# RWKV-7 features: the key norm's root, turn and spreads moved between the gate sigmoids, with one PSUM place for the spreads

## What is computed

```python
w_log = -jax.nn.softplus(-(w0 + jnp.einsum('bldr,drc->bldc', jnp.tanh(lw), w2))) - 0.5
decay = jnp.exp(-jnp.exp(w_log))
a = jax.nn.sigmoid(a0 + jnp.einsum('bldr,drc->bldc', la, a2))
gate = jax.nn.sigmoid(lg) @ g2
kk = l2_normalize(heads(k * k_k))          # t * rsqrt(sum(t*t) + eps), per head of 64 channels
k_dir = k[:, :, None, :] * (1.0 + (a - 1.0) * k_a)
...
y = y + jnp.sum(r * k_dir[:, :, d] * u[d], axis=-1, keepdims=True) * v     # the bonus, d = 0, 1
```

## Time and profile before

| | |
|---|---|
| median of 3 runs | 4022.79 us (4021.42 to 4027.47) |
| profiled execution | 4033.49 us |
| its span in the trace | 4031.8 us |
| PE busy | 3817.7 us (95%) |
| DVE busy | 2206.8 us (55%) |
| ACT busy | 1455.2 us (36%) |
| POOL busy | 760.1 us (19%) |

### The profile page before, as it was taken

How to read it: one execution, slowest core, us unless ns; L and a number is a source line. 1 busy time by engine, 2 the same in 40 slices (tenths; PEclk the granted TensorE clock), 3 DMA queues, 4 the chain that set the end, 5 groups by cost and what they waited for, 6 DMA issues and landing times. The chain is left out here.

```text
span 4031.8 us, 93050 instructions
## 1 busy us (share of the span) xinstructions
PE 3817.7 (95%) x40211; PEld 3336.3 (83%) x40211; DVE 2206.8 (55%) x3770; ACT 1455.2 (36%) x2510; POOL 760.1 (19%) x879
## 2 busy tenths in 40 slices
PE   7999999999988888999999999999999988889999
PEld 5899998878867767999998999987887867758887
DVE  4655556466464444755556655566565464444444
ACT  4333334343353333433334333343333253333232
POOL 1222210043023310222211222200232043300000
PEclk9999999999999999999999999999999999999999
DMA  6433332100200021323223333332100200032332
GB/s 214 126 119 105 105 102 74 37 13 2 77 11 4 5 70 43 113 87 99 87 66 116 107 113 105 105 105 58 28 2 17 71 2 5 5 110 80 88 112 66
DMA packets 409036, 287.20 MB, mean 71 GB/s; under 512 B 13438, under 2 KB 366180, under 8 KB 408164
## 3 DMA queue, kind: packets, MB, share of 16 engines
q1 hardware_dynamic: 408676, 281.86, 22.9%
HBM read 270.27 MB, written 11.53 MB: 70 GB/s over the span
## 5 line engine op out<-in xcount | busy, mean ns | idle before, releaser
L804 ACT ACTIVATE w_hi<-w_raw 128x512 fp32r<-128x512 f32 (+1 forms) x724 | 406.0, 613 | 645.0 <-POOL w_raw L788 347.9
L811 DVE TENSOR_TENSOR w_lo<-w_raw,w_hi 128x512 fp32r<-128x512 f32 (+1 forms) x724 | 484.9, 710 | 170.7 <-ACT w_hi L804 170.7
L919 PE MATMUL PS<-x_hi,w_hi 128*128 128x384 f32 x1680 | 562.4, 335 | 1.4 <-DVE hid_flat L1106 1.4
L919 PE MATMUL PS<-x_lo,w_hi 128*128 128x384 f32 x1680 | 561.3, 334 | 0.0
L919 PE MATMUL PS<-x_hi,w_lo 128*128 128x384 f32 x1680 | 561.2, 334 | 0.0
L1191 DVE SCALAR_TENSOR_TENSOR arena<-PS,mod,arena 128x256 f32<-128x256 f32 (+1 forms) x336 | 198.4, 632 | 332.5 <-PE PS L932 332.3
L1106 DVE TENSOR_TENSOR hid_flat<-hid_flat,PS 128x384 f32<-128x384 f32 (+1 forms) x454 | 246.1, 557 | 239.5 <-PE PS L919 153.1
L932 PE MATMUL PS<-hidden_hi,w_hi 128*128 128x256 f32 (+1 forms) x1232 | 341.7, 347 | 7.7 <-DVE hidden_lo L1158 5.7
L932 PE MATMUL PS<-hidden_lo,w_hi 128*128 128x256 f32 (+1 forms) x1232 | 336.9, 343 | 0.0
L932 PE MATMUL PS<-hidden_hi,w_lo 128*128 128x256 f32 (+1 forms) x1232 | 336.7, 343 | 0.0
L781 POOL TENSOR_TENSOR w_raw<-w_raw 128x512 f32<-128x512 f32 x60 | 86.3, 1438 | 1271.1 <-DMA w_raw<-in_ffn_w_dram 1186.8
(11 more groups left out here) (359 smaller groups left out, 7402.1 us busy)
## 6 DMA issues: line engine op xcount, KB each, us to landing
w_raw<-in_ffn_w_dram SPq DMA_DIRECT2D x512, 256.0 KB, 4.0
arena<-in_ada_w_dram SPq DMA_DIRECT2D x120, 512.0 KB, 5.8
arena<-in_w_in_dram SPq DMA_DIRECT2D x64, 512.0 KB, 3.9
arena<-in_ada_w_dram SPq DMA_DIRECT2D x6, 2048.0 KB, 14.7
arena<-in_w_out_dram SPq DMA_DIRECT2D x16, 512.0 KB, 4.3
h_save<-arena SPq DMA_DIRECT2D x16, 384.0 KB, 2.7
arena<-h_save SPq DMA_DIRECT2D x2, 3072.0 KB, 16.6
w_raw<-in_ffn_w_dram SPq DMA_DIRECT2D x32, 128.0 KB, 2.3
```

The source lines that it names most:

```text
L804: nc.scalar.activation(w_hi[:, high_place(n, what, j), 0:size], w_raw[:, load_of[what] % 2, place, 0:size], ACT.Copy).then_inc(w_high_read ...
L811: nc.vector.tensor_tensor(w_lo[:, b, place, 0:size], w_raw[:, b, place, 0:size], w_hi[:, high_place(n, what, j), 0:size].bitcast(F32), ALU ...
L919: mm = pe.matmul(PS[:, 4 * b + bank, 0:half], w[wo], x_split[xo][:, j, k, 0:half], start=(k == 0 and q == 0), stop=(k == KH - 1 and q == 2))
```

## The change

Five edits, once for each layer.

- ACT: the root of the key norm is taken right after `square(3)`, behind the gates of tile 0, and no longer behind those of tile 3. The four `widen` stand between later gates. `begin_bonus(0)`, (1) and (2) come later by one or two places.
- PE: the four `sum_squares` stand in one row ahead of `lora(1, 0)`; the turn stands behind `lora(1, 1)`; `spread(0)` to `spread(3)` stand ahead of `lora(2, 0)`, `lora(2, 1)`, `lora(3, 0)` and `lora(3, 1)`; all four `sum_bonus` come last.
- All spreads go to `RSTD`, so `spread(j)` waits for `normalize(j - 1)` from j = 1 on; before, it waited from j = 2 on for `normalize(j - 2)`.
- DVE: the inversion stands behind `scan(0, 1)`, the normalizations between the scans, `bonus(1)` and (2) one place or more later, `take_bonus(0)` ahead of `bonus(3)`.
- The counts of the semaphore `fe_dve` follow the new order.

```diff
-            for j in range(NB):
-                for d in range(2):
-                    gates(j, d)
-                if j == 0:
-                    square(2)
-                    square(3)
-                else:
-                    begin_bonus(j - 1)
-                if j == NB - 2:
-                    sc.activation(lora_g, lora_g, ACT.Sigmoid)
+            gates(0, 0)
+            gates(0, 1)
+            square(2)
+            square(3)
             act.wait_ge(kk_summed, K0(layer) + NB)
             sc.activation(fsq_rows, RSTD[0:8, :], ACT.Sqrt, bias=eps[0:8, 0:1]).then_inc(kk_rooted, 1)
-            begin_bonus(NB - 1)
+            gates(1, 0)
             act.wait_ge(kk_step, (1 + 2 * NB) * layer + NB + 1)
             widen(0)
             widen(1)
+            gates(1, 1)
+            begin_bonus(0)
+            gates(2, 0)
+            widen(2)
+            gates(2, 1)
+            begin_bonus(1)
+            widen(3)
+            sc.activation(lora_g, lora_g, ACT.Sigmoid)
+            gates(3, 0)
+            gates(3, 1)
+            begin_bonus(2)
+            begin_bonus(3)
             act.wait_ge(fe_dve, scanned(layer, NB - 1, 1))
...
-            widen(2)
-            widen(3)
...
-                if j >= 2:
-                    pe.wait_ge(kk_step, (1 + 2 * NB) * layer + NB + j)
+                if j >= 1:
+                    pe.wait_ge(kk_step, (1 + 2 * NB) * layer + NB + 1 + j)
...
-                    mm = pe.matmul(KK_PLACE[j % 2][:, t * P:(t + 1) * P], fsq[:, j % 2, t * P:(t + 1) * P], ident[:, :],
+                    mm = pe.matmul(RSTD[:, t * P:(t + 1) * P], fsq[:, j % 2, t * P:(t + 1) * P], ident[:, :],
...
-            for j in range(1, NB):
-                if j < 3:
-                    sum_squares(2 * j - 2)
-                    sum_squares(2 * j - 1)
-                for d in range(2):
-                    lora(j, d)
+            sum_squares(0)
+            sum_squares(1)
+            sum_squares(2)
+            sum_squares(3)
+            lora(1, 0)
+            lora(1, 1)
             pe.wait_ge(kk_rooted, 2 * layer + 2)
             pe_head_turn(pe, fsq_rows).then_inc(qk_summed, 1)
-            sum_bonus(0)
-            sum_bonus(1)
             spread(0)
+            lora(2, 0)
             spread(1)
+            lora(2, 1)
             spread(2)
+            lora(3, 0)
             spread(3)
-            sum_bonus(2)
-            sum_bonus(3)
+            lora(3, 1)
+            pe.wait_ge(gates_ready, WAYS * (layer + 1))
+            for j in range(NB):
+                sum_bonus(j)
...
-            for j in range(NB):
+            for j in range(2):
                 for d in range(2):
                     scan(j, d)
-                if j > 0:
-                    bonus(j - 1)
-            dve.wait_ge(qk_summed, (layer + 1) * HEAD_STEPS)
-            dve_head_invert(dve).then_inc(kk_step, 1)
-            bonus(NB - 1)
+                if j == 0:
+                    dve.wait_ge(qk_summed, (layer + 1) * HEAD_STEPS)
+                    dve_head_invert(dve).then_inc(kk_step, 1)
+            bonus(0)
             normalize(0)
+            scan(2, 0)
             normalize(1)
+            scan(2, 1)
+            normalize(2)
+            bonus(1)
+            scan(3, 0)
+            normalize(3)
+            scan(3, 1)
+            bonus(2)
             take_bonus(0)
-            take_bonus(1)
-            normalize(2)
-            normalize(3)
-            take_bonus(2)
-            take_bonus(3)
+            bonus(3)
+            for j in range(1, NB):
+                take_bonus(j)
```

More of the change, by code:

```diff
@@ L2249, in bonus_made @@
         def bonus_made(layer, j, n):
-            return FE_DVE * layer + (fe_before(j + 1) + 2 if j < NB - 1 else fe_before(NB) ) + n
+            return FE_DVE * layer + (fe_before(j + 1) + 2 if j < NB - 1 else fe_before(NB) + 1) + n
         def bonus_taken(layer, j):
-            return FE_DVE * layer + fe_before(NB) + 2 + j + 1
+            return FE_DVE * layer + fe_before(NB) + (1 if j == 0 else 3 + j)
         def sp_lora(sp, layer):
@@ L2404, in normalize @@
                 dve.wait_ge(kk_spread, K0(layer) + i + 1)
-                mult(KK[:, i, :], KK[:, i, :], KK_PLACE[i % 2]).then_inc(kk_step, 1)
+                mult(KK[:, i, :], KK[:, i, :], RSTD).then_inc(kk_step, 1)
             def take_bonus(j):
```

## The result

| | before | changed |
|---|---|---|
| median | 4025.13 us (4 runs) | 4052.91 us (4046.75 to 4057.72, 4 runs) |
| ratio, 95% interval | 1 | 1.0067 (1.0053 to 1.0081) |
| profiled execution, its span | 4033.49, 4031.8 us | 4051.05, 4049.3 us |
| first sigmoid to first product of the recurrence, layer 0 | 48.62 us | 61.55 us |
| the same, layer 1 | 48.05 us | 65.06 us |

The time is 27.8 us above before by the medians, and 4044 was forecast. The two feature stages are 12.9 + 17.0 = 29.9 us longer in the profiled execution, so the loss lies where the prediction put it.

What follows compares the result with a forecast made beforehand. PE waits in the feature stage, whose keys_on_b(0) starts 48.62 us behind ACT's first sigmoid, with DVE late. Order +8.6 and clock 2 x (3.9 + 2.3) make +21.0 on 4022.8, so 4044 us; range 4028 to 4055.

Steps and rivals of the forecast that it cites:

- rival D: All gaps fall into the lower clock in both layers, or the added table load shows: 4050 to 4058, chance 0.09.
- ACT's slack of 5.3 us at its last gates: ACT runs 5.3 us ahead of DVE there, so gates 13.2 late make the last scan 7.9 later; sign 8 to 12.
- Table loads hidden: ACT's loads around the early root hide in waits; the added one would otherwise cost 1.28 us per layer.
- The order terms: Delay of the feature stages at full clock: +4.0 us in layer 0, +4.6 in layer 1, sum +8.6.
- the ring: PE's products queue behind spread(1), which waits for normalize(0) in DVE's queue; ACT waits 5.1 us for lora(2, 1).
- The tail of 12.7: From the last scan to keys_on_b(0): 12.7 us, between 11.3 and 13.5, instead of 16.6.
- The clock term: Half speed on PE per layer: 3.9 us in spread(1) and lora(2, 1), 2.3 around the bonus sums.
- The gap ahead of `spread(1)`: PE idles 4.6 us there; a second spread within 3 us of the product before it would make the prediction wrong.
- A cost left at nothing: PE's waits ahead of sum_squares(2), 2 us and 3.7 us by layer, could cost up to 4 more; nothing taken.
- Part 1: Root moved behind tile 0: ACT falls about 6.5 us behind its old time, eating its 5.3 of slack.
- Rival A: PE's clock stays up and only the ring costs: +8.6 us, 4031.4, chance 0.22.
- Rivals B and C: B: ring hides in the slack, 4015, chance 0.05. C: ring late by 9 to 12 us, 4019 to 4028, 0.07.

Runs made afterwards that it cites:

- e4: Changed kernel with ACT.Identity in place of the key norm's root, so that two table loads are gone: ratio 1.0064.
- e9: Changed kernel with filler matmuls in PE's gaps, the one behind the turn included, and no order changed: ratio 1.0037, median 4041.44 us.
- e6: Kernel before with only the root, turn, inversion and first two widens moved early, spreads and normalizations as before: ratio 1.0034.
- e10: Changed kernel run once more, unaltered: ratio 1.0085, median 4061.78 us.
- e3: Changed kernel with filler matmuls ahead of sum_squares(2), spread(1) and three bonus sums, none in the gap behind the turn: ratio 1.0049.

## Why the prediction was right, and where not

The direction and the place were right, and the size is inside the range: 4044 forecast, 4052.9 measured, 4028 to 4055 stated, +21.0 us against +27.8. But the measured time lies above the forecast's own band (4037 to 4050) and in that of rival D (4050 to 4058, chance 0.09), and the range held it because it took in half of D. Step by step:

- **ACT's slack of 5.3 us at its last gates: right for the changed kernel.** These gates begin 19.3 and 26.3 us later than before, and the last scan ends 14.0 and 20.7 later, 5.3 and 5.6 less. That is more than the 8 to 12 us given as a sign.
- **Table loads hidden: right** (e4, and 0.58 us idle behind the second load in layer 0).
- **The order terms: right.** 8.6 us at full clock was the sum, 10.5 is what e9 shows, its fillers included. The wait of ACT in the ring, 5.1 foreseen, is 4.96 in e9. The tail of 12.7 is 12.9 in e9 and in layer 1 of the changed kernel; its terms as listed reach 12.7 only with the upper figure for `bonus(3)`, and 12.3 with the middle.
- **The clock term: mis-sized.** I took 6.2 us per layer and e9 shows 7.8 and 11.6. I took 3.9 of it ahead of the last scan and 2.3 behind; by e9 it is 5.2 and 2.6 in layer 0, and 11.6 and nothing in layer 1. The step that failed is where the clock falls and how long it stays down. I put the fall into a gap of 4.6 us ahead of `spread(1)` and let it slow two pieces, `spread(1)` and `lora(2, 1)`. It falls one gap sooner, in or right behind the 1.71 us behind the turn, in both layers. In layer 1 it then stays down from `spread(0)` to `spread(3)`, seven pieces. In layer 0 it comes back for `lora(2, 0)` (2.99 us) and falls again in the gap foreseen; there `spread(1)` and `lora(2, 1)` take 8.39 us against 4.42 in e9, 4.0 more where 3.9 was foreseen, but `spread(2)` is slow as well.
- **The gap ahead of `spread(1)`.** At full clock it is as foreseen: in e9 `lora(2, 0)` ends 4.1 us ahead of `spread(1)`. In the changed kernel the slow pieces fill most of it, and 2.61 and 0.60 us are left. I had written that a second spread within 3 us of the product before it would make the prediction wrong. By that mark its account of this gap was wrong, though the wait of ACT behind it (7.4 and 5.4 measured) was there.
- **A cost left at nothing.** For the gap ahead of `sum_squares(2)` I took nothing. In layer 1 it is 3.67 us, the sums behind it take 5.29 us instead of 2.75, and the root comes 11.5 us behind the first sigmoid, against 9.2 in layer 0. That price stood among the rivals (D) and belonged in the sum.
- **Part 1 underrated.** I let the early root's 6.5 us eat the slack of 5.3 and no more. That slack exists only at the last gates. At tile 1 DVE has none, and in e6 the early root alone costs 6.1 and 8.4 us.
- **Rival A** (the clock stays up, +8.6) is what e9 makes by hand, +10.5 in the distances. **Rivals B and C** needed the ring to hide, and it didn't.

## What to carry to other kernels

A step moved out of the tail into a chain of short waits is paid for by whoever is queued behind each wait. Count the late engine's slack first, at the place where the step goes in and not at the end, and look whether the same tail can be shortened on the engine that is late anyway: one inversion moved ahead of the last scan and `bonus(2)` won 4 us in the two stages, where the large reordering lost 30. And where a change cuts PE's work into pieces with waits between, price every piece at half speed, the ones ahead of the long gap too.

## What the runs showed of the hardware

Behind a gap of 1.71 us after six tiny matmuls TensorE's clock went from its upper level (2.4 GHz) to the lower (1.2), in both layers of the changed kernel and again in e10. In layer 1 the granted clock is 1.00 from 3261 to 3264 and 0.50 from 3266.4 to 3272. Filler instructions in earlier and later gaps alone did not prevent it (e3); 12 more in this gap did (e9). The length of the gap alone doesn't decide it: behind 1.78 us ahead of the first bonus sums the changed kernel ran on at full speed in both layers (2.85 us for two sums).

And the clock does not come back as soon as PE is at work again. From 3264 to 3291 PE is busy 26.4 of 27 us with spreads and products, and the granted clock of the stretch is 0.51:

```profile
3264.00:3291.00 27.00, 26.38 (x69) 16.92 (x70) 14.30 (x12) 14.44 (x18) 8.79 (x4) 0.51 0.00 1
```

In layer 0 the same instructions saw it come back twice: during `lora(2, 0)` (0.94 from 1185.5 to 1188.5), before it fell again, and by 1203. Why one recovers and the other doesn't isn't settled by these runs.
